# Another order in the mix and routing stage of a hybrid attention and expert kernel: the last w_mix group's chunks ahead of biases and tables, routers 1 and 2 ahead of block 3's turn, the weights in one set

## What is computed

```
h = h + hybrid_mixer(rmsnorm(h, norm_mix_g))      # its last step: merged @ w_mix_out
hn = rmsnorm(h, norm_ffn_g)
logits = hn @ router_w + router_b                  # 512 x 32
top_v, top_e = top_k(logits, 4); gates = softmax(top_v)
for each expert e, its tokens in blocks of up to 128 (place = rank of the token in e):
    x = hn[tokens] @ w_gate_up[e] + b_gate_up[e]
    act = (clip(up) + 1) * gate * sigmoid(1.702 * gate)
    h[tokens] += gates * (act @ w_down[e] + b_down[e])
out = rmsnorm(h, norm_final_g)
```

## Time and profile before

| | us |
|---|---|
| median of 3 runs | 1967.07 |
| lowest and highest | 1964.32, 1970.83 |
| the profiled execution's own time | 1971.95 |
| its span | 1970.1 |
| mean granted clock of TensorE, share of full speed | 0.971 |
| TensorE, VectorE, ScalarE, POOL busy | 1864.8, 1443.7, 1125.7, 144.6 |
| DMA | 490.04 MB, mean 249 GB/s |

### The profile page before, as it was taken

One profiled execution on the slowest core, in us unless ns is written; L12 is line 12 of the kernel. 1 busy time (PEld: TensorE's weight loads), 2 busy tenths in 40 slices (PEclk: granted clock), 3 DMA queues, 4 the chain that ended last, 5 costly groups with the idle time before them and its releaser, 6 DMA issues. The chain is left out here.

```text
span 1970.1 us, 25039 instructions
## 1 busy us (share of the span) xinstructions
PE 1864.8 (95%) x8962; PEld 1523.8 (77%) x8963; DVE 1443.7 (73%) x1388; ACT 1125.7 (57%) x1003; POOL 144.6 (7%) x95
## 2 busy tenths in 40 slices
PE   7999999999999976999999999999999999999973
PEld 5777788987788765888888888888878888878862
DVE  3146344347333456999999999999999999999982
ACT  4343222245432235777777777777777777777761
POOL 0000000000000000011010010110110100100101
PEclk9999999999999977999999999999999999999996
DMA  5211222311033465999999999999999999999952
GB/s 199 85 64 64 82 85 85 100 37 52 22 107 140 119 258 193 344 363 360 361 365 367 365 361 357 371 355 363 366 360 358 367 364 371 363 351 367 362 202 91
DMA packets 99510, 490.04 MB, mean 249 GB/s; under 512 B 15504, under 2 KB 17296, under 8 KB 50048
## 3 DMA queue, kind: packets, MB, share of 16 engines
q1 hardware_dynamic: 89952, 471.92, 64.0%
q0 software_dynamic: 9216, 16.81, 3.6%
q10 hardware_dynamic: 288, 0.59, 0.1%
HBM read 482.96 MB, written 23.07 MB: 257 GB/s over the span
## 5 line engine op out<-in xcount | busy, mean ns | idle before, releaser
L1551 DVE TENSOR_TENSOR expert_lo<-expert_chunk,expert_hi 128x2048 fp32r<-128x2048 f32 x384 | 866.3, 2289 | 55.8 <-ACT expert_hi L1546 55.4
L1546 ACT CAST expert_hi<-expert_chunk 128x2048 fp32r<-128x2048 f32 x384 | 735.1, 1916 | 250.9 <-PE psum L1644 215.7
L236 DVE TENSOR_TENSOR chunk_lo<-chunk,chunk_hi 128x2048 fp32r<-128x2048 f32 x48 | 109.9, 2290 | 268.4 <-ACT chunk_hi L232 268.4
L1641 PE MATMUL psum<-expert_hi,rowsT_hi 128*128 128x512 f32 x1024 | 285.6, 401 | 0.0
L1641 PE MATMUL psum<-expert_hi,rowsT_lo 128*128 128x512 f32 x1024 | 274.9, 390 | 0.0
L1644 PE MATMUL psum<-expert_lo,rowsT_hi 128*128 128x512 f32 x1024 | 274.3, 390 | 0.0
L1641 PEld LDWEIGHTS psum<-expert_hi,rowsT_lo 128*128 128x128 f32 x1024 | 192.8, 188 | 41.8
L1644 PEld LDWEIGHTS psum<-expert_lo,rowsT_hi 128*128 128x128 f32 x1024 | 192.2, 188 | 40.7
L1641 PEld LDWEIGHTS psum<-expert_hi,rowsT_hi 128*128 128x128 f32 x1024 | 186.3, 189 | 45.8 <-issue 12.3
L267 PE MATMUL psum<-chunk_hi,xT_hi 128*128 128x512 f32 x480 | 191.8, 400 | 16.6 <-DVE h_sb L1398 11.4
L232 ACT CAST chunk_hi<-chunk 128x2048 fp32r<-128x2048 f32 x48 | 91.7, 1910 | 187.7 <-PE psum L267 169.2
(11 more groups left out here) (249 smaller groups left out, 2062.7 us busy)
## 6 DMA issues: line engine op xcount, KB each, us to landing
expert_chunk<-in_expert_w_gate_up SPq DMA_DIRECT2D x256, 1024.0 KB, 7.7
expert_chunk<-in_expert_w_down SPq DMA_DIRECT2D x128, 1024.0 KB, 7.2
chunk<-in_w_in SPq DMA_DIRECT2D x38, 1024.0 KB, 5.1
chunk<-in_w_branch_gla SPq DMA_DIRECT2D x4, 1024.0 KB, 5.0
chunk<-in_w_mix_out SPq DMA_DIRECT2D x4, 1024.0 KB, 4.9
gla_v<-in_x SPq DMA_DIRECT2D x4, 512.0 KB, 6.9
chunk<-in_w_branch_att SPq DMA_DIRECT2D x2, 1024.0 KB, 4.9
h_sb<-in_x SPq DMA_DIRECT2D x1, 2048.0 KB, 9.8
```

The lines of the kernel that those rows point to most:

```text
L236: dve.tensor_tensor(self.wlo[c][:], self.raw[c][:], self.whi[c][:].bitcast(F32), ALU.subtract).then_inc(self.lo_done[c], 1)
L1546: act.copy(whi[c % SLOTS][:], raw[c % RING][:]).then_inc(S["hi"], 1)
L1551: dve.tensor_tensor(wlo[s][:], raw[c % RING][:], whi[s][:].bitcast(F32), ALU.subtract).then_inc(S["lo"], 1)
L1641: pe.matmul(bank, x[:, k, :], whi[s][:, m // 2, m % 2 * COLS:(m % 2 + 1) * COLS], start=False, stop=False)
```

## The change

Five pieces of one stage's lists are put in another order, and one step is done once for several blocks.

- SP: the load of the last w_mix group's chunk 1 goes ahead of the bias and table loads, and the seven bias loads go ahead of the three tables that stood in front of them.
- ScalarE: both chunks of the last group are split ahead of the two bias copies.
- VectorE: the low parts of the biases and the preparation of the tables go from in front of chunk 0's low part to behind chunk 1's, which is ahead of the second additions.
- TensorE: turn(2) goes ahead of router(1), and router(2) ahead of turn(3).
- Weights: `weigh(b, n)` does n blocks at once, as five instructions in place of four. It is called for block 0 ahead of `add(3, 1)`, and for blocks 1 to 3 behind `choose(3)`, which itself goes ahead of the wait for the ranks. `weight_rows` of blocks 1 to 3 wait for all four blocks.

```diff
--- before.py
+++ after.py
@@ -1146,22 +1146,22 @@
                 self.load_group(sp, base_mix, self.chunk_of(w_mix, 0))
                 sp.wait_ge(self.lo_done[0], last_mix)
                 sp.dma_start(self.raw[0][:], self.chunk_of(w_mix, COLS)(0)).then_inc(self.loaded[0], 16)
+                sp.wait_ge(self.lo_done[1], last_mix)
+                sp.dma_start(self.raw[1][:], self.chunk_of(w_mix, COLS)(1)).then_inc(self.loaded[1], 16)
 
                 sp.wait_ge(S["merged_lo"], KT)
-                sp.dma_start(raw_before[:], t["before"]).then_inc(R["in"], 16)
-                sp.dma_start(tok[:], t["token_numbers"]).then_inc(R["in"], 16)
-                sp.dma_start(self.slot_no[:], t["slot_numbers"]).then_inc(R["in"], 16)
                 for n in range(4):
                     sp.dma_start(raw_bias[n * E:(n + 1) * E, :], t["expert_b_gate_up"][0]).then_inc(R["bias_in"], 16)
                 for n in range(3):
                     sp.dma_start(raw_down[n * E:(n + 1) * E, :], t["expert_b_down"][0]).then_inc(R["bias_in"], 16)
+                sp.dma_start(raw_before[:], t["before"]).then_inc(R["in"], 16)
+                sp.dma_start(tok[:], t["token_numbers"]).then_inc(R["in"], 16)
+                sp.dma_start(self.slot_no[:], t["slot_numbers"]).then_inc(R["in"], 16)
                 sp.dma_start(g[:], t["norm_ffn_g"][0:1, :].partition_broadcast(P).rearrange("p a n -> p (a n)")).then_inc(R["in"], 16)
                 sp.dma_start(rw[:], t["router_w"][0].rearrange("(k p) n -> p k n", p=P)).then_inc(R["in"], 16)
                 sp.dma_start(rb[:], t["router_b"][0:1, :].partition_broadcast(P).rearrange("p a n -> p (a n)")).then_inc(R["in"], 16)
                 sp.dma_start(e_no[:], t["expert_numbers"]).then_inc(R["in"], 16)
                 sp.dma_start(self.bias_row[:], t["bias_row"]).then_inc(R["in"], 16)
-                sp.wait_ge(self.lo_done[1], last_mix)
-                sp.dma_start(self.raw[1][:], self.chunk_of(w_mix, COLS)(1)).then_inc(self.loaded[1], 16)
                 for k in range(6):
                     self.load_gate_up(sp, k, 0, k)
                 sp.wait_ge(R["bias_lo"], 3)
@@ -1256,10 +1256,10 @@
                 mix_block(0, 3)
                 turn(1)
                 mix_block(1, 3)
+                turn(2)
                 router(1)
-                turn(2)
+                router(2)
                 turn(3)
-                router(2)
                 router(3)
                 pe.wait_ge(R["prepared"], 2)
                 pe.wait_ge(R["selected"], 3)
@@ -1289,11 +1289,11 @@
                     self.split_hi(act, g, 1)
                     if g > base_gla:
                         self.merged_hi(act, S, merged, g - 1 - base_gla)
+                self.split_hi(act, last_mix, 0)
+                self.split_hi(act, last_mix, 1)
                 act.wait_ge(R["bias_in"], 7 * 16)
                 act.copy(bias[:], raw_bias).then_inc(R["bias_hi"], 1)
                 act.copy(down_bias[:], raw_down).then_inc(R["bias_hi"], 1)
-                self.split_hi(act, last_mix, 0)
-                self.split_hi(act, last_mix, 1)
 
 
                 def square(b, i):
@@ -1317,7 +1317,7 @@
                     act.activation(ex_all[:, b, :], logits[:, b, :], ACT.Exp, bias=low[:, b:b + 1]).then_inc(R["exps"], 1)
 
                 def weight_rows(b):
-                    act.wait_ge(R["pairs"], 2 * b + 2)
+                    act.wait_ge(R["pairs"], 4 if b else 1)
                     for n, part_ in enumerate((1, 1, 2)):
                         act.copy(self.weight_rows[:, b, n, :], self.pairs[:, b, :, part_].bitcast(F32))
 
@@ -1374,23 +1374,7 @@
                             self.merged_lo(dve, S, merged, m - 1)
                     self.merged_lo(dve, S, merged, m)
                 link = self.link("dve", dve)
-                dve.wait_ge(R["bias_hi"], 2)
-                for n in (1, 3):
-                    low_rows = slice(n * E, (n + 1) * E)
-                    dve.tensor_tensor(bias[low_rows, :], raw_bias[low_rows, :], bias[low_rows, :].bitcast(F32),
-                                      ALU.subtract).then_inc(R["bias_lo"], 1)
-                low_rows = slice(E, 2 * E)
-                dve.tensor_tensor(down_bias[low_rows, :], raw_down[low_rows, :], down_bias[low_rows, :].bitcast(F32),
-                                  ALU.subtract).then_inc(R["bias_lo"], 1)
                 self.split_lo(dve, last_mix, 0)
-                dve.wait_ge(R["in"], 8 * 16)
-                dve.wait_ge(R["half_set"], 2)
-                dve.tensor_copy(before[:], raw_before[:]).then_inc(R["prepared"], 1)
-                dve.tensor_copy(ones[:], raw_ones[:]).then_inc(R["prepared"], 1)
-                link(dve.tensor_scalar(self.slot_no[:], self.slot_no[:], 1.0, None, ALU.add))
-                all_tokens = tok[:].unsqueeze(2).to_broadcast([P, NB, E])
-                link(dve.tensor_scalar(self.pairs[:, :, :, 0], all_tokens, 1.0, None, ALU.add))
-                link(dve.tensor_scalar(self.pairs[:, :, :, 3], all_tokens, 0.0, None, ALU.mult))
 
                 def add(b, i):
                     dve.wait_ge(self.bank_full[b], base_mix + i + 1)
@@ -1424,16 +1408,16 @@
                             link(last)
                     last.then_inc(R["selected"], 1)
 
-                def weigh(b):
-                    dve.wait_ge(R["exps"], 2 * b + 2)
-                    link(dve.reciprocal(tot[:, b:b + 1], tot[:, b:b + 1]))
-                    dve.wait_ge(R["selected"], b + 1)
-                    link(dve.scalar_tensor_tensor(out=wsum[:, b, :], in0=ex_all[:, b, :], scalar=tot[:, b:b + 1],
-                                                  in1=sel[:, b, :].bitcast(F32), op0=ALU.mult, op1=ALU.mult))
-                    dve.tensor_copy(self.pairs[:, b, :, 1], wsum[:, b, :]).then_inc(R["pairs"], 1)
-                    dve.wait_ge(R["pairs"], 2 * b + 1)
-                    dve.tensor_tensor(self.pairs[:, b, :, 2], wsum[:, b, :], self.pairs[:, b, :, 1].bitcast(F32),
-                                      ALU.subtract).then_inc(R["pairs"], 1)
+                def weigh(b, n):
+                    at = slice(b, b + n)
+                    dve.wait_ge(R["exps"], 2 * (b + n))
+                    link(dve.reciprocal(tot[:, at], tot[:, at]))
+                    dve.wait_ge(R["selected"], b + n)
+                    link(dve.tensor_tensor(wsum[:, at, :], ex_all[:, at, :], tot[:, at].unsqueeze(2).to_broadcast([P, n, E]), ALU.mult))
+                    link(dve.tensor_tensor(wsum[:, at, :], wsum[:, at, :], sel[:, at, :].bitcast(F32), ALU.mult))
+                    link(dve.tensor_copy(self.pairs[:, at, :, 1], wsum[:, at, :]))
+                    dve.tensor_tensor(self.pairs[:, at, :, 2], wsum[:, at, :], self.pairs[:, at, :, 1].bitcast(F32),
+                                      ALU.subtract).then_inc(R["pairs"], n)
 
                 def rank(bank, blocks):
                     n = len(blocks)
@@ -1445,6 +1429,22 @@
                 for b in range(NB):
                     add(b, 0)
                 self.split_lo(dve, last_mix, 1)
+                dve.wait_ge(R["bias_hi"], 2)
+                for n in (1, 3):
+                    low_rows = slice(n * E, (n + 1) * E)
+                    dve.tensor_tensor(bias[low_rows, :], raw_bias[low_rows, :], bias[low_rows, :].bitcast(F32),
+                                      ALU.subtract).then_inc(R["bias_lo"], 1)
+                low_rows = slice(E, 2 * E)
+                dve.tensor_tensor(down_bias[low_rows, :], raw_down[low_rows, :], down_bias[low_rows, :].bitcast(F32),
+                                  ALU.subtract).then_inc(R["bias_lo"], 1)
+                dve.wait_ge(R["in"], 8 * 16)
+                dve.wait_ge(R["half_set"], 2)
+                dve.tensor_copy(before[:], raw_before[:]).then_inc(R["prepared"], 1)
+                dve.tensor_copy(ones[:], raw_ones[:]).then_inc(R["prepared"], 1)
+                link(dve.tensor_scalar(self.slot_no[:], self.slot_no[:], 1.0, None, ALU.add))
+                all_tokens = tok[:].unsqueeze(2).to_broadcast([P, NB, E])
+                link(dve.tensor_scalar(self.pairs[:, :, :, 0], all_tokens, 1.0, None, ALU.add))
+                link(dve.tensor_scalar(self.pairs[:, :, :, 3], all_tokens, 0.0, None, ALU.mult))
                 dve.wait_ge(R["squared"], NB)
                 dve.tensor_scalar(ss[:, :, 0], ss[:, :, 0], 1.0 / D_MODEL, EPS, ALU.mult, ALU.add).then_inc(R["early"], 1)
                 add(0, 1)
@@ -1457,18 +1457,16 @@
                 mean(2)
                 norm(2)
                 choose(0)
+                weigh(0, 1)
                 add(3, 1)
                 mean(3)
                 norm(3)
-                weigh(0)
                 choose(1)
                 choose(2)
-                weigh(1)
-                weigh(2)
+                choose(3)
+                weigh(1, 3)
                 dve.wait_ge(R["ranks"], 1)
                 rank(self.bank[4], (0, 1, 2))
-                choose(3)
-                weigh(3)
```

## The result

| | before | changed |
|---|---|---|
| median of 6 runs, us | 1971.32 (1964.32 to 1973.64) | 1958.54 (1955.94 to 1962.94) |
| profiled execution's own time, its span, us | 1971.95, 1970.1 | 1962.94, 1960.8 |
| mean granted clock | 0.971 | 0.974 |

The ratio of the means is 0.9943, with a 95% interval of 0.9924 to 0.9963: 11.2 us faster (7.3 to 15.0); the two medians alone would say 12.8. The forecast of 1953.4, made from a median of 1967.07, was 13.7 us faster. The direction and the place were right. The runs alone can't tell 13.7 from 11.2, but the traces can: there the size was 2.4 us too large.

The account below looks back on a forecast made before the run. TensorE, busy 1864.8 of 1970.1 us, was taken as the bound, with an 11.37 us stop before the last w_mix group. Terms -12.3 - 0.5 - 0.9 = -13.7 from the median 1967.07 gave 1953.4 us, range 1948.8 to 1960.

Parts of the forecast that it names:

- Chunks first: Last w_mix group: splitting its chunks ahead of biases removes TensorE's stop and clock loss, saving 11.4 and 2.65, together 14.0 us.
- Biases and tables behind them: VectorE's moved work of 7.2 us, 5.5 under TensorE's blocks: 1.9 us wait ahead of turn(0), net so far -12.3 us.
- Landing of the biases: SP's queue: 1 MB of w_mix now ahead of the biases delays them 0 to 1.2 us; 0 taken.
- Rival C: Slower: biases land behind the expert loads and hold up additions and turns; 1976 us if served last; chance 0.03.
- turn(0) to M: Stretch from turn(0) to M, the end of block (1,3): forecast difference 0, before 12.02 us.
- rival B: Clock falls at the new wait ahead of turn(0), or biases come late: gain 9.5 to 12, about 1956.5 us; chance 0.19.
- weigh(0) ahead of block 3's addition: VectorE behind block (1,3): addition starts 1.0 us after that block's end instead of at it; router(2) can start at 3.6.
- Routers 1 and 2 ahead of turn(3): TensorE behind block (1,3): last router ends 11.6 us after it instead of 12.15, clock falling again; gain 0.5 us.
- Rival A: The tail behind block (1,3) keeps 2.4 GHz and ends 2.6 us earlier than forecast: 1950.8 us; chance 0.12.
- Weights in one set: Last router to the first expert list: 5.9 us instead of 6.8, ranks running beside; gain 0.9 us.

Follow-up runs that it names:

- e9: Changed kernel with SP's load order of before: chunk 1's load of the last w_mix group behind biases and tables; ratio 0.9969, stage 50.4 us.
- e3: Changed kernel with one bias row and the table operations moved from ahead of the second additions to behind norm(1); ratio 0.9931, stage 44.1 us.
- e4: Changed kernel with 8 matmuls that nobody reads put into TensorE's wait ahead of turn(0); ratio 0.9931, stage 44.3 us.
- e5: e3 with block 0's weights moved back behind norm(3), as before the change; ratio 0.9936, stage 42.4 us.
- e14: The kernel before, with nothing changed, profiled a second time; stage 55.9 us.
- e13: e5 with TensorE's order of before behind block (1,3): router(1), turn(2), turn(3), router(2), router(3); ratio 0.9918, stage 41.7 us.
- e1: Changed kernel with the tail of before, so only the chunks-first half of the change; ratio 0.9948, stage 45.6 us.
- e10: e1 profiled once more, nothing else changed; stage 45.5 us.
- e7: e5 with ScalarE copying turn(2) out ahead of block 3's square, plus unread matmuls at eight places in TensorE's waits; ratio 0.9924, stage 41.6 us.
- e8: e7 with the old tail order, weights block by block and block 3 chosen behind the ranks; ratio 0.9929, stage 43.9 us.

## Where the prediction held, and which step failed

*Chunks first* was right to 0.1 us: the stop of 11.4 us, its clock, and turn(0) 12.3 us earlier (12.2). Its cover was right as well: chunk 1's low part was ready at 692.8, before block (1,0) wanted it at 693.9.

*Biases and tables behind them* was right: the bias copies run straight behind chunk 1, the second additions at 700.36, the wait of 1.9 us (2.03). *Landing of the biases* cost nothing, the value taken: the last one landed at about 687.1, 1.5 us later than before, and its copy came only at 690.35. Rival C never came near. e9 shows what the moved load is worth.

The step that failed is the one that isn't in the sum: **turn(0) to M** was put at no difference, and the clock's fall behind the new stop was left to rival B. It happened in every trace that has a stop of 2 us or more there, for 1.6 us; e3 and e4 settle it. The argument against it, that blocks follow at once, was wrong: the clock had fallen 0.8 us into turn(0), before they could help. The prediction had itself named a clock of 0.50 between 700 and 706 as a sign of being wrong, and the first list at 732.3 as one of being right; the list came at 735.91, of which 1.3 us lie ahead of the stage. Of the times given, B's, about 1956.5, is the one nearest to the runs, and its gain of 9.5 to 12 us takes in the 11.2 measured.

The 2.4 us that the stage fell short of the forecast are these 1.6, 0.6 in the tail, and 0.1 each in the first and the last part.

*weigh(0) ahead of block 3's addition* was right in its mechanism (M + 0.9 instead of M + 1.0, router(2) at M + 3.4), and too small in its weight: it was priced as something that the shorter order pays for, and e5 shows 1.65 us in the tail from moving it back, at the same fall.

*Routers 1 and 2 ahead of turn(3)*, a gain of 0.5 by the forecast, gained nothing against that trace of before (+0.1), and against the tail that the old order has in five of its six traces it loses 2.4 to 3.1 us (9.31 to 9.85 against 12.25 to 12.42). The forecast took the fall at M + 3.9 for a property of the tail; in all traces but that one a fall near M + 4 comes with the new order. Why the new order brings it forward isn't shown. Rival A, a tail at 2.4 GHz, was ruled out by this, too.

*Weights in one set*: 0.84 of the 0.9 us, in each of the traces with it.

Taken together, against the second trace of before (e14, stage 55.9) the change gains 8.4 us in its stage, and chunks first alone 10.3. So 2.9 of the 11.3 us rest on which trace of before is taken, and that the total came as near as it did is luck to that extent. Which of the two tails before has more often two traces can't say. The runs can't tell the two kernels apart: 0.9943 and 0.9948, each with 0.0015 to 0.002 to either side.

## What to carry to other kernels

When a stop of the bounding engine is taken away, look at what the moved work now stands in front of: 7 us of side work fitted under 5.5 us of cover, and the 2 us that stuck out cost 3.6, since the clock fell behind them. Split such work to the size of the holes that the trace shows (e3 did; e13, built on it, has a stage 5.8 us shorter than the change). And take a second trace of the kernel before a forecast rests on the moment at which a clock falls: here two traces of before differ by 2.9 us in this one stage.

## What was not expected

The granted clock fell within turn(0) behind 2.03 us of idleness (changed kernel, five traces with e1 and e10) and behind 2.73 us (e9), and not behind 0.2 us and the same turn (e3, e4 and the later kernels); the price was 1.5 to 1.6 us each time. Two orders of the same five steps behind M, turns 2 and 3 and routers 1 to 3, differ in the moment of the fall, 4.0 to 4.4 against 7.5 to 7.7 us behind it, with one exception on either side. Full-width matmuls in the waits kept the clock at 2.4 GHz through some 27 us in which it had been at 1.2 without them (e7), but where the clock was low in spite of them they took 2.48 us instead of 1.41 for five and overran the waits (e8).
